# Every fourth weight block of the second half, while expert rows are gathered, loaded as two transfers of 104 and 24 partitions

## The chip, the cores and the metric

The kernel runs on one core of one Trainium2 chip. The metric is device time in microseconds of one execution; the median of three executions before the change is 2417.49 us (2416.55 to 2422.78).

## The reference

Two transformer layers in float32 on one sequence of 512 positions, width 1024. The first mixes with a gated delta rule and sparse attention, followed by a gated feed-forward part with a short convolution (width 2816). The second mixes with a pooling and a convolution branch, and then has an expert layer, which decides what follows here:

```python
q = (hc @ w_query).reshape(PEER_CHUNK, PEER_HEADS, PEER_KEY_DIM)      # 8 heads
...
experts = jnp.take_along_axis(cand_idx, pos, axis=-1)                 # 16 of 16384 per head
gate = jax.nn.softmax(top_s.astype(jnp.float32), axis=-1).astype(hc.dtype)
u = jnp.take(expert_u, experts, axis=0)
act = jax.nn.gelu(jnp.einsum('chkd,cd->chk', u, hc))
v = jnp.take(expert_v, experts, axis=0)
return jnp.einsum('chk,chkd->cd', gate * act, v)
```

Each of the 512 positions picks 8 x 16 = 128 experts, and of each the two rows u and v of 1024 floats are used. That is 512 x 128 x 8 KB = 537 MB to be read.

## The kernel before, in words

Positions are taken in two halves of 256. The first half runs ahead through the dense work of both layers; from about 940 us on the core gathers expert rows for its positions, and does the dense work of the second half (feed-forward up and down, `w_in_2`, `branch`, `w_out_2`, `query`) beside it.

The gather. `expert_u` and `expert_v` lie side by side in `experts`, so one indirect transfer brings for each of 128 positions one row of 8 KB, one row to each partition: 1 MB, 128 packets of 8 KB. There are 512 of them (4 tiles of 128 positions x 128 picks), issued by GpSimd in the last loop of its program (L2814) into `ring_e`, a ring of `RING` = 9 buffers. GpSimd waits before each until the row that had the buffer is used. A landed buffer is dotted with the position's vector on VectorE (`row_dot`, L2622), ScalarE makes the weight from it (L1761 to L1773), and the row is then summed on TensorE (`row_pair`) or, for some, on VectorE (`side_row`). Rows are taken in pairs; a pair is a step `p` of 0 to 255.

The dense blocks. `weight_order()` writes out by hand the order in which TensorE takes the weight blocks of the second half: block `t` of 0 to 191 is `ORDER[t]`, and `TURN` is the inverse. Which block stands after which pair is set by `UP_AT`, `DOWN_AT`, `WIN_AT`, `BRANCH_AT`, `WOUT_AT` and `QUERY_AT`. A block is 128 partitions x 1024 floats (512 KB), for eight of the `down` blocks 128 x 768 (384 KB). SyncE (SP) issues the loads in the order of `t` (L586 for `down`, L588 for the rest) into three slots (`SLOTS2` = 3, the tile `w2` in `ring`); slot `t % 3` is loaded again once TensorE has done block `t - 3` (`half_done`). TensorE waits in `weights(name, s, m)` on `slot_ready[t % 3]`, which each transfer raises by 16, before the block's matmuls. Blocks from 59 on belong to the steps of the gather.

TensorE's program is one sequence: for each pair first `row_pair(p, ...)` and then `beside(p)`, which holds the dense blocks. So a block that is late holds up the rows behind it, and a row that is late the blocks.

Of the kernel before, what the change touches and what calls it, by code (L numbers as in the profile page):

```python
# [32 lines left out]
SLOTS = 4  # L33
# [40 lines left out]
FIRST = {}  # L74
# [6 lines left out]
SLOTS2 = 3  # L81
# [64 lines left out]
def weight_order():  # L146

    order = [("w_out", 1, m) for m in range(SLOTS, KT)]
    order += [("w_in_2", 0, m) for m in range(28)] + [("branch", 0, m) for m in range(KT)]
    order += [("w_out_2", 0, m) for m in range(KT)] + [("up", 1, 0), ("up", 1, 1)]  # L150
    order += [("query", 0, m) for m in range(EARLY)] + [("up", 1, 2)]
    for p in range(NC * TILE):
        order += [("query", 0, m) for m, q in QUERY_AT[0].items() if q == p]
        order += [("up", 1, b) for b, q in enumerate(UP_AT) if q == p]
        order += [("down", 1, d) for d, q in enumerate(DOWN_AT) if q == p]
        order += [("w_in_2", 1, m) for m, q in enumerate(WIN_AT) if q == p]
        order += [("branch", 1, m) for m, q in enumerate(BRANCH_AT) if q == p]
        order += [("w_out_2", 1, m) for m, q in enumerate(WOUT_AT) if q == p]
        order += [("query", 1, m) for m, q in QUERY_AT[1].items() if q == p]
    return order  # L160


ORDER = weight_order()
TURN = {b: t for t, b in enumerate(ORDER)}


class Count:
# [29 lines left out]
def build(nc, a, out):  # L197
    ctx = ExitStack()
    with ctx:
# [106 lines left out]
        w2 = wring[:, 0:SLOTS2 * D].rearrange("p (j n) -> p j n", n=D)  # L306
# [61 lines left out]
        def sem(name):  # L368
            return ctx.enter_context(nc.semaphore(name))
# [135 lines left out]
        slot_ready = [sem(f"slot{j}_ready") for j in range(SLOTS)]  # L505
# [12 lines left out]
        def evicted(t):  # L518

            name, half, m = ORDER[t]  # L520
            if name == "w_out":
                return x1_ready, KT + m + 1
            if name == "w_in_2":
                return sg_ready, 28 * half + m + 1
            if name == "branch":
                return m_half, KT * half + m + 1
            if name == "w_out_2":
                return x3_ready, KT * half + m + 1
            if name == "up":
                return fy_ready, 2 * FT + m + 1  # L530
            if name == "down":
                return x2_ready, KT + m + 1
            return q_ready, 16 * half + m + 1
# [8 lines left out]
        def bank(name, half, m):  # L542
            if name == "w_out":
                return (4, 5, 6, 0)[m - SLOTS]
            return 2 + TURN[name, half, m] % SLOTS2

# [3 lines left out]
        @block.sync  # L550
        def _(sp):
            first = STREAM[0]
            sp.dma_start(crow, a["crow"][0]).then_inc(params_loaded, 16)
            sp.dma_start(const[:, 0:HEAD_CONST], a["const"][:, 0:HEAD_CONST]).then_inc(inputs_loaded, 16)
            sp.dma_start(xT[:], a["x"]).then_inc(inputs_loaded, 16)
            sp.dma_start(param[:], a["param"]).then_inc(rows_loaded, 16)
            sp.wait_ge(ada_used, 8)
            for j in range(SLOTS):
                sp.dma_start(ring[:, j, :D], a["w_in"][j]).then_inc(slot_ready[j], 16)
            sp.dma_start(const[:, HEAD_CONST:], a["const"][:, HEAD_CONST:]).then_inc(rest_loaded, 16)  # L560
            sp.dma_start(mats[:], a["mats"]).then_inc(rest_loaded, 16)
            for name, blocks, width in STREAM:
                lo = 1 if name == first[0] else 0
                with sp.Fori(lo, blocks // SLOTS) as i:
                    for j in range(SLOTS):

                        sp.wait_ge(blocks_done, FIRST[name] + i * SLOTS + j - SLOTS + 1)
                        if name == "down":
                            src = a[name][bass.ds(i * 2 + j // 2, 1)].rearrange("o p n -> p (o n)")[:, (j % 2) * WIDE:(j % 2 + 1) * WIDE]
                        else:  # L570
                            src = a["w_out" if name == "w_out_again" else name][bass.ds(i * SLOTS + j, 1)].rearrange("o p n -> p (o n)")
                        sp.dma_start(ring[:, j, :width], src).then_inc(slot_ready[j], 16)
            for t, (name, half, m) in enumerate(ORDER):

                if (name, half, m) == ("query", 1, KT):
                    sp.wait_ge(fin_ready, 1)
                    sp.dma_start(out[0], prow).then_inc(out_done, 16)

                if t < SLOTS2:
                    sp.wait_ge(blocks_done, FIRST["down"] + 13 + t)  # L580
                else:
                    sp.wait_ge(half_done, t - SLOTS2 + 1)
                if name == "down":
                    c, k = divmod(m, KT)
                    lo, hi = c * CHUNK * P, min(FT, (c + 1) * CHUNK) * P
                    sp.dma_start(w2[:, t % SLOTS2, 0:hi - lo], a[name][k][:, lo:hi]).then_inc(slot_ready[t % SLOTS2], 16)  # L586
                else:
                    sp.dma_start(w2[:, t % SLOTS2, :], a[name][m]).then_inc(slot_ready[t % SLOTS2], 16)  # L588
            for c in range(1, NC - 1):

                sp.wait_ge(fin_ready, c + 1)
                sp.dma_start(out[c], prow).then_inc(out_done, 16)
            for v in range(2):

                sp.wait_ge(fin_ready, NC + 1 + v)
                sp.dma_start(out[NC - 1][:, v * S:(v + 1) * S], prow[:, v * S:(v + 1) * S]).then_inc(out_done, 16)
            sp.wait_ge(out_done, 16 * (NC + 1))
# [3 lines left out]
        def _(pe):  # L601
# [280 lines left out]
            for c in range(NC):  # L882
                t = slice(c * P, (c + 1) * P)
# [125 lines left out]
            def weights(name, s, m):  # L1009

                t = TURN[name, s, m]
                pe.wait_ge(slot_ready[t % SLOTS2], 16 * (FIRST["down"] // SLOTS + 4 + t // SLOTS2 + 1))
                if t >= SLOTS2:
                    pe.wait_ge(*evicted(t - SLOTS2))
                return [w2[:, t % SLOTS2, k * P:(k + 1) * P] for k in range(KT)]

            def project_rest(m, lo=0, hi=KT):

                w = weights("w_out", 1, m)
                if m == KT - 1:  # L1020
                    pe.wait_ge(x2_ready, SLOTS + 1)
                for k in range(lo, hi):
                    ins = mm(PS[:, bank("w_out", 1, m), :HF], w[k], mix[:, k, HF:], k == 0, k == KT - 1)
                if hi == KT:
                    ins.then_inc(half_done, 1)

            def expand(m, lo=0, hi=KT):

                w = weights("up", 1, m)
                if m == 0:  # L1030
                    pe.wait_ge(h_ready, KT * 4)
                for k in range(lo, hi):
                    ins = mm(PS[:, bank("up", 1, m), :HF + 2], w[k], hf[:, k, :], k == 0, k == KT - 1)
                if hi == KT:
                    ins.then_inc(half_done, 1)

            def contract(c, m):

                w = weights("down", 1, c * KT + m)
                tiles_ = min(CHUNK, FT - c * CHUNK)  # L1040
                if m == 0:
                    pe.wait_ge(ff_ready, FT + c * CHUNK + tiles_)
                for k in range(tiles_):
                    ins = mm(PS[:, bank("down", 1, c * KT + m), :HF], w[k], gc[:, c % 2, k, :], k == 0, k == tiles_ - 1)
                ins.then_inc(half_done, 1)
# [47 lines left out]
            def branch_conv(s, m):  # L1093

                t = TURN["branch", s, m]
                if m == 0:
# [217 lines left out]
        def _(act):  # L1314
# [271 lines left out]
            def keep_block(s, m):  # L1586

                act.wait_ge(half_done, TURN["w_in_2", s, m] + 1)
                src = PS[:, bank("w_in_2", s, m), :HF]
# [56 lines left out]
            def up_tap(m):  # L1646

                t, z = divmod(m, 2)
                act.wait_ge(half_done, TURN["up", 1, m] + 1)
                if t >= 2:  # L1650
# [31 lines left out]
            def keep_query(s, m):  # L1682

                act.wait_ge(half_done, TURN["query", s, m] + 1)
                if 16 * s + m >= 2:
# [1256 lines left out]
```

## Time and profile before

| | us |
|---|---|
| median of three executions | 2417.49 (2416.55 to 2422.78) |
| the profiled execution's own time | 2412.99 |
| its span, first to last instruction | 2411.3 |
| TensorE busy | 2082.3 (86%) |
| VectorE busy | 1679.4 (70%) |
| ScalarE busy | 861.5 (36%) |
| GpSimd busy | 634.9 (26%) |
| expert rows moved by the gather, queue q0 (with other loads of GpSimd) | 588.90 MB |
| SyncE's transfers, queue q1 | 163.84 MB |

The profile gives for any stretch the busy time of each engine, the mean busy share of the core's 16 DMA engines and the bytes that they moved. A DMA share of 1.00 is all 16 busy; 0.06 is one of 16. Three kinds of queue matter: q0 is what GpSimd issues (here the expert rows), q1 what SyncE issues (here the weight blocks), q8 and q14 carry the program's own instructions to the engines.

### The profile page before, as it was taken

The page shows a single profiled execution, that of the slowest core. Times are in us where ns is not written, and L with a number is a line of the kernel's source. Part 1 is how long each engine was busy: PE and PEld are TensorE (multiplying, and loading weights), DVE is VectorE, ACT ScalarE, POOL GpSimd, SP SyncE. Part 2 cuts the span into 40 slices and gives each one's busy share as a digit, 9 for nine tenths or more (in the row PEclk, how much of TensorE's full clock was granted, in tenths as well). Part 3 has the DMA queues.
Part 4 walks back from the last instruction along what each step waited for, and adds up shares of the span by engine and source line. Part 5 has one row for each costly group of instructions (what it writes and reads, how often), then busy time and mean ns, then how long its engine had stood idle before and what let it go on. Part 6 is the DMA issues. An engine that isn't in the chain of part 4 may idle for free.

```text
span 2411.3 us, 26498 instructions
## 1 busy us (share of the span) xinstructions
PE 2082.3 (86%) x8832; PEld 1483.9 (62%) x8832; DVE 1679.4 (70%) x3760; ACT 861.5 (36%) x2094; POOL 634.9 (26%) x606
## 2 busy tenths in 40 slices
PE   7999998899999998999986878787788878777776
PEld 3444787788888887877765666676644423322322
DVE  5563645476657737999998999876676666676654
ACT  2321345421103213423326446356643333342332
POOL 2100000000110002333344334344444443444442
PEclk9999998999999999999997989899799999999999
DMA  8631120266774348999999999999999999999997
GB/s 350 197 121 55 34 71 1 105 225 228 259 282 147 133 157 326 412 417 415 418 416 420 407 379 402 399 398 420 420 420 421 421 421 422 419 421 419 421 422 292
DMA packets 131790, 754.31 MB, mean 313 GB/s; under 512 B 14544, under 2 KB 14672, under 8 KB 65616
## 3 DMA queue, kind: packets, MB, share of 16 engines
q0 software_dynamic: 87456, 588.90, 60.0%
q1 hardware_dynamic: 44208, 163.84, 18.7%
q8 instruction: 66, 1.08, 0.2%
q14 instruction: 60, 0.49, 0.1%
HBM read 750.59 MB, written 2.10 MB: 312 GB/s over the span
## 4 chain that ended last, share of the span: by engine, by line
PE 43%; DMA 31%; DVE 16%; ACT 5%; issue 3%; POOL 0%; DVEq 0%; SPq 0%; ACTq 0%; POOLq 0%
PE PS L603 41%; DMA arena<-experts_dram,ecur 25%; DVE arena L2622 5%; DVE arena L1891 4%; DVE h_all L1891 2%; DMA ring<-down_dram 2%; PE PS L1149 2%; DVE ring L1891 1%; DMA ring<-up_dram 1%; DVE arena L1885 1%; ACT L1761 1%; ACT arena L1765 1%; ACT arena L1771 1%; ACT const L1773 1%; DMA ring<-query_dram 1%
## 5 line engine op out<-in xcount | busy, mean ns | idle before, releaser
L603 PE MATMUL PS<-h_all,ring 128*128 128x256 f32 (+2 forms) x3584 | 895.9, 408 | 18.2 <-DMA ring<-up_dram 6.1
L2814 POOL DMA_INDIRECT arena<-experts_dram,ecur x512 | 585.8, 1144 | 1092.7 <-PE PS L1149 385.6
L2622 DVE CUSTOM_DVE_ANT_0 arena<-arena 128x1024 f32<-128x1024 f32 x512 | 626.1, 1223 | 282.8 <-DMA arena<-experts_dram,ecur 279.7
L603 PEld LDWEIGHTS PS<-h_all,ring 128*128 128x128 f32 x3584 | 681.1, 193 | 208.3 <-issue 102.8
L603 PE MATMUL PS<-arena,const 128*128 128x512 f32 (+1 forms) x1056 | 497.0, 618 | 135.7 <-ACT const L1773 125.1
L603 PEld LDWEIGHTS PS<-arena,const 128*128 128x128 f32 x1056 | 198.4, 196 | 418.5 <-issue 220.3
L1149 PE MATMUL PS<-const,arena 128*128 128x128 f32 x1304 | 196.6, 308 | 117.3 <-ACT arena L1771 113.4
L1761 ACT ACTIVATE arena<-arena 128x2 f32<-128x2 f32 x255 | 51.6, 202 | 659.4 <-DVE arena L2622 659.0
L1149 PEld LDWEIGHTS PS<-const,arena 128*128 128x128 f32 x1304 | 171.6, 159 | 143.4 <-ACT arena L1771 125.6
L603 PE MATMUL PS<-arena,ring 128*128 128x256 f32 x1088 | 245.9, 384 | 13.3 <-DMA ring<-down_dram 7.3
L603 PEld LDWEIGHTS PS<-arena,ring 128*128 128x128 f32 x1088 | 205.9, 192 | 47.8 <-DMA ring<-down_dram 12.8
L1771 ACT ACTIVATE arena<-arena 128x1024 f32<-128x1024 f32 x161 | 177.6, 1134 | 0.0
L603 PE MATMUL PS<-arena 128*128 128x128 f32 (+4 forms) x936 | 137.7, 299 | 8.4 <-DVE arena L1885 3.4
L603 PEld LDWEIGHTS PS<-arena 128*128 128x128 f32 (+2 forms) x936 | 117.9, 194 | 28.9 <-issue 12.8
L1891 DVE SCALAR_TENSOR_TENSOR arena<-arena 128x1024 f32<-128x1024 f32 (+3 forms) x132 | 125.8, 953 | 2.4
L1942 DVE CUSTOM_DVE_ANT_0 arena<-arena 128x1024 f32<-128x1024 f32 x92 | 108.9, 1222 | 25.1 <-DMA arena<-ada_dram 23.8
L1765 ACT ACTIVATE arena<-arena 128x1 f32<-128x1 f32 x510 | 122.4, 287 | 8.4
L1891 DVE SCALAR_TENSOR_TENSOR arena<-PS,param,arena 128x255 f32<-128x255 f32 (+3 forms) x128 | 72.3, 565 | 42.5 <-ACT arena L1392 31.6
L1891 DVE SCALAR_TENSOR_TENSOR xT<-PS,mod,xT 128x256 f32<-128x256 f32 x71 | 34.2, 482 | 79.9 <-PE PS L603 79.3
L1773 ACT ACTIVATE const<-const,arena 128x128 f32<-128x128 f32 x254 | 86.2, 387 | 0.0
L2794 POOL DMA_DIRECT2D arena<-crow_dram x1 | 0.5, 528 | 315.9 <-ACT arena L1556 315.9
L2801 POOL DMA_DIRECT2D arena<-ada_dram x44 | 23.2, 528 | 222.3 <-DVE mod L1942 209.5
(279 smaller groups left out, 1659.8 us busy)
## 6 DMA issues: line engine op xcount, KB each, us to landing
ring<-up_dram SPq DMA_DIRECT2D x88, 512.0 KB, 3.4
ring<-w_in_dram SPq DMA_DIRECT2D x80, 512.0 KB, 4.1
arena<-ada_dram POOLq DMA_DIRECT2D x80, 512.0 KB, 5.2
ring<-w_out_dram SPq DMA_DIRECT2D x32, 512.0 KB, 4.9
ring<-query_dram SPq DMA_DIRECT2D x32, 512.0 KB
ring<-down_dram SPq DMA_DIRECT2D x16, 704.0 KB, 5.9
ring<-branch_dram SPq DMA_DIRECT2D x16, 512.0 KB
arena<-experts_dram,ecur POOLq DMA_INDIRECT x512
```

The source lines that it names most:

```text
L603: return nc.tensor.matmul(o, l, r, start=start, stop=stop)
L1149: ins = nc.tensor.matmul(PS[:, k // 4, (k % 4) * P:(k % 4 + 1) * P], row[:, k * P:(k + 1) * P], ident, start=start and k % 4 == 0, stop=st ...
L1761: A(wts[:, b, :], dots[:, b, :], ACT.Gelu_apprx_tanh).then_inc(gelu_ready, 1)
L1765: A(wts[:, b, k:k + 1], wts[:, b, k:k + 1], ACT.Copy, scale=gcur[:, r % 3, j:j + 1]).then_inc(w_ready2, 1)
L1771: A(row, row, ACT.Copy, scale=wts[:, b, k:k + 1]).then_inc(row_scaled, 1)
L1773: A(diag[:, b, k, :], ident, ACT.Copy, scale=wts[:, b, k:k + 1]).then_inc(diag_ready if k == rows[-1] else act_step, 1)
L1885: return V.tensor_tensor(out=o, in0=x, in1=y, op=op)
L1891: return V.scalar_tensor_tensor(out=o, in0=x, scalar=s_, in1=y, op0=op0, op1=op1)
L1942: V.tensor_tensor_reduce(out=w, in0=w, in1=row, scale=1.0, scalar=0.0, op0=MUL, op1=ADD, accum_out=mod[:, blk, t:t + 1]).then_inc(used, 1)
L2622: V.tensor_tensor_reduce(out=u, in0=u, in1=hrow[:, (r // HEADS) % 2, :], scale=1.0, scalar=0.0, op0=MUL, op1=ADD, accum_out=dots[:, p % NB ...
L2801: pool.dma_start(ring_2[:, j, :], a["ada_2"][bass.ds(i * SLOTS + j, 1)].rearrange("o p n -> p (o n)")).then_inc(slot_2_ready[j], 16)
L2814: nc.gpsimd.indirect_dma_start(out=ring_e[:, g % RING, :], out_offset=None, in_=a["experts"], in_offset=bass.IndirectOffsetOnAxis(ap=ecur[ ...
```

## The change

A weight block with `t >= 59` and `t % 4 == 0` is loaded by two transfers, one for the partitions 0 to 103 and one for 104 to 127, into the same slot. Both raise the slot's semaphore by 16, and TensorE waits for the sum of all transfers of that slot so far. That is so for the 33 blocks t = 60, 64, ..., 188 of the 133 blocks from 59 on. Bytes, slots, the order of blocks and what TensorE does with them stay as they were.

```diff
+HEAD_PART = 104
+FIRST_SPLIT, EVERY = 59, 4
+
+
+def split(t):
+
+    return t >= FIRST_SPLIT and t % EVERY == 0
+
+
+def weight_landed(t):
+
+    return 16 * sum(1 + split(u) for u in range(t % SLOTS2, t + 1, SLOTS2))
...
-                    sp.dma_start(w2[:, t % SLOTS2, 0:hi - lo], a[name][k][:, lo:hi]).then_inc(slot_ready[t % SLOTS2], 16)
+                    w, src = w2[:, t % SLOTS2, 0:hi - lo], a[name][k][:, lo:hi]
                 else:
-                    sp.dma_start(w2[:, t % SLOTS2, :], a[name][m]).then_inc(slot_ready[t % SLOTS2], 16)
+                    w, src = w2[:, t % SLOTS2, :], a[name][m]
+                if split(t):
+                    sp.dma_start(w[0:HEAD_PART], src[0:HEAD_PART]).then_inc(slot_ready[t % SLOTS2], 16)
+                    sp.dma_start(w[HEAD_PART:], src[HEAD_PART:]).then_inc(slot_ready[t % SLOTS2], 16)
+                else:
+                    sp.dma_start(w, src).then_inc(slot_ready[t % SLOTS2], 16)
...
-                pe.wait_ge(slot_ready[t % SLOTS2], 16 * (FIRST["down"] // SLOTS + 4 + t // SLOTS2 + 1))
+                pe.wait_ge(slot_ready[t % SLOTS2], 16 * (FIRST["down"] // SLOTS + 4) + weight_landed(t))
```

## Rows read from the trace of the kernel before

**Rows 1.** Busy time by stretch: engines' busy us (instructions), TensorE clock, DMA share, GB/s.

```profile
940.00:1260.00 320.00, 291.39 (x1398) 244.58 (x1398) 299.04 (x620) 112.68 (x277) 115.57 (x91) 0.98 1.02 416
1260.00:1390.00 130.00, 95.28 (x500) 82.17 (x501) 117.07 (x275) 68.41 (x134) 48.56 (x44) 0.87 1.01 414
1390.00:1650.00 260.00, 204.97 (x1119) 178.50 (x1118) 225.12 (x529) 136.66 (x269) 106.56 (x85) 0.89 0.99 397
1650.00:1850.00 200.00, 157.34 (x673) 110.87 (x672) 132.89 (x340) 103.03 (x241) 83.00 (x72) 0.89 1.01 421
1850.00:2390.00 540.00, 421.83 (x950) 176.08 (x949) 354.85 (x859) 177.76 (x598) 223.62 (x213) 0.97 1.01 421
```

**Rows 2.** The DMA queues, 940 to 1260 us: packets, MB, share of 16 engines.

```profile
DMA packets 23701, 133.10 MB, mean 416 GB/s; under 512 B 2634, under 2 KB 2634, under 8 KB 12042
q0 software_dynamic: 13090, 95.34, 72.1%
q1 hardware_dynamic: 10590, 37.49, 29.1%
q8 instruction: 11, 0.18, 0.2%
```

**Rows 3.** The queues of SyncE and of the instructions, 1260 to 1390 us.

```profile
q1 hardware_dynamic: 2096, 7.60, 14.6%
q8 instruction: 4, 0.07, 0.2%
```

**Rows 4.** The same, 1390 to 1650 us.

```profile
q1 hardware_dynamic: 4751, 17.30, 16.7%
q8 instruction: 9, 0.15, 0.2%
```

**Rows 5.** The same, 1650 to 2390 us.

```profile
q1 hardware_dynamic: 2017, 7.34, 2.5%
q8 instruction: 13, 0.21, 0.1%
```

**Rows 6.** Busy time by stretch, the end of the gather, columns as in rows 1.

```profile
2380.00:2390.00 10.00, 6.66 (x15) 2.88 (x16) 5.00 (x9) 2.54 (x10) 2.30 (x2) 1.00 1.01 421
2390.00:2392.00 2.00, 0.74 (x2) 0.00 (x0) 0.77 (x3) 1.27 (x5) 0.00 (x0) 1.00 0.51 213
2392.00:2393.00 1.00, 0.99 (x3) 0.52 (x4) 1.00 (x1) 0.00 (x0) 0.00 (x0) 1.00 0.16 66
2393.00:2394.00 1.00, 1.00 (x4) 0.52 (x3) 0.09 (x2) 0.00 (x0) 0.00 (x0) 1.00 0.06 25
...
2398.00:2399.00 1.00, 1.00 (x4) 0.48 (x3) 0.03 (x2) 0.87 (x3) 0.00 (x0) 1.00 0.04 16
```

**Rows 7.** The queues, 2393.5 to 2399.2 us.

```profile
q0 software_dynamic: 20, 0.14, 5.9%
```

**Rows 8.** Instructions of VectorE's line L2622, 2370 to 2402 us, and what they waited for.

```profile
L2622 DVE CUSTOM_DVE_ANT_0 arena<-arena x12: 1224/1225/1226, 2371.0 to 2399.3; 128x1024 f32<-128x1024 f32 x12
...
  DMA arena<-experts_dram,ecur: 15.9, 12
```

**Rows 9.** Who waited for whom, 940 to 1260 us: us in total, times, longest.

```profile
POOL arena L2814 <- PE PS L1149: 164.9, 27, 16.9
...
PEld PS L603 <- DMA ring<-up_dram: 15.8, 22, 1.9
...
PEld PS L603 <- DMA ring<-down_dram: 12.8, 14, 1.8
...
```

**Rows 10.** SyncE's line L588, 940 to 1900 us: duration ns min/median/max.

```profile
L588 SPq DMA_DIRECT2D ring<-up_dram x39: 327/328/328, 955.1 to 1181.4; - x39
```

**Rows 11.** The chain that ended last, in order of time: start, us, what.

```profile
955.10 9.29 DMA ring<-up_dram
...
1646.38 16.92 DMA arena<-experts_dram,ecur
...
2396.95 6.29 PE PS L603 x14
```

## The prediction

> **What bounds the kernel now.** I read first the busy time by stretch [rows 1]. The reader is to see that from 940 us on the DMA engines are the full resource: share 1.01 to 1.02 and 414 to 421 GB/s in four stretches, and only 1390 to 1650 us has some air, with 397 GB/s. No other engine is full throughout: TensorE has 291 of 320 us in the first stretch and 422 of 540 in the last, VectorE 225 of 260 us in the middle one. The chain that ended last says the same [rows 11]: early on it goes through loads of weight blocks (9.3 us the one at 955 us), later through landings of expert rows (16.9 us the one at 1646 us).
>
> A mean share can hide that the 16 engines are not equally loaded, so next I read the end of the gather, where no new rows are issued [rows 6]. Up to 2390 us all 16 are busy. In 2390 to 2392 the share is 0.51, in the next microsecond 0.16, and from 2393 to about 2398.7 it is 0.06 or less at 25 GB/s: one engine of sixteen, alone for about 6 us, with 20 packets left [rows 7]. So one engine is some 6 us behind the rest, and the last rows wait for it: VectorE waited before each of its last 12 dot products for rows, 15.9 us in total, the last of them starts at 2399.3 [rows 8], and TensorE's last piece of 6.3 us ends behind it [rows 11].
>
> Why one? Every transfer of rows or weights ends with 16 small packets (2634 under 512 B over 91 gathers and 73 loads in 940 to 1260 us is 16.06 each [rows 2]; GpSimd's 91 instructions are the gathers [rows 1]), so all 16 engines take part in each and get 128/16 = 8 rows. What isn't spread is the instruction traffic: q8 had 11, 4, 9 and 13 packets of 16 KB in the four stretches [rows 2 to 5], 37 in all, of which each is one packet and so on one engine. The first 11 took 0.2% of 16 x 320 us, so about 0.93 us each (0.7 to 1.2 with the rounding). If all are on one engine it carries some 34 us more than the rest. At the end only 6 us of lag are left from the last 13 (12 us), since wherever the rest idle the late one catches up; 1390 to 1650 us is such a place. I take 6/13 = 0.46 us of lag per fetch as an estimate for the first stretches as well.
>
> **The change part by part.** SyncE's bytes in the four stretches [rows 2 to 5], at 0.524 MB a block (0.393 for eight, and 1.57 MB of results going out in the last), are some 73, 14, 32 and 11 loads. Counted back from the last block that is t = 62 to 191. So split ones are 18 in the first, 4 in the second, 8 in the third and 2 in the fourth; t = 60 is just before.
>
> *Issue.* Each split costs SyncE one more instruction of 0.33 us [rows 10], 33 x 0.33 = 11 us in all. SyncE has nothing but some 130 such issues in 900 us and waits for TensorE's blocks between them, so nothing is queued that this makes late; only the split block's second part starts 0.33 us later.
>
> *Packets.* A row of a block stays one packet of 4 KB, so 128 as before, with 16 more small ones. In 940 to 1260 us q1 took 29.1% of 16 x 320 us = 1490 us for 37.49 MB, that is 0.163 us per 4 KB packet; q0 took 72.1% for 95.34 MB, 0.317 us per 8 KB packet [rows 2].
>
> *Who moves them.* Neither 104 nor 24 divides by 16, so the load can't stay equal. The trace has no such transfer. Bounds: as evenly as it goes, an engine gets 7 + 2 = 9 rows at most in place of 8; at 8 rows an engine, as in a whole block, the 104 rows take 13 engines, and the 24 rows fall with 2 or 3 each on the first of the same, so 10 or 11 rows there and none on three engines. I take 10 rows on the busy ones and none on three, since 8 rows an engine is what the whole blocks have. Then a split adds 2 x 0.163 = 0.33 us to most engines and takes 8 x 0.163 = 1.3 us off three.
>
> The Trainium skill, page DMA: Bandwidth & Descriptors, section "Why a DMA increments its semaphore by 16 and not by 1", says that the number of engines is the largest one up to 16 that divides the outer dimension, the lowest-numbered ones: 13 for 104 rows and 12 for 24. By that rule engines 0 to 11 get 10 rows, engine 12 gets 8 and engines 13 to 15 none. No run here shows it yet.
>
> *940 to 1390 us.* DMA is full. 22 splits cost most engines 22 x 0.33 = 7.2 us (0 to 10.8 between no and three extra rows). The late engine has by then 15 fetches x 0.46 = 6.9 us of lag. If it is one of the three left out, it loses 22 x 1.3 = 29 us of work, lands with or before the rest, and the rest are 7.2 - 6.9 = 0.3 us later than the late one was. I take +0.3 us.
>
> *1390 to 1650 us.* 397 of 421 GB/s leaves 6% of 260 us, 15 us of air on each engine [rows 1], against 8 x 0.33 = 2.6 us: 0. If the cover were gone, +2.6 us.
>
> *From 1650 us.* Two splits. Most engines +0.65 us, which lies inside the 6 us in which they are idle at the end; the late one, if left out, 2 x 1.3 = 2.6 us less: -2.6 us, as its lag is what the end waits for.
>
> Sum: +0.3 + 0 - 2.6 = -2.3 us, on 2412.99 us of the profiled execution (its span and 1.7 us around it) 2410.7. The median of the runs lies 4.5 us above that execution, so in the terms of the median 2417.5 - 2.3 = 2415.2 us.
>
> **The rivals.** (a) *The late engine keeps its rows.* If it is one of those that get 10 rows, both the full stretches and the end are paid: 22 x 0.33 + 2 x 0.33 = +7.9 us, 2425.4 us. For it: twelve or thirteen of sixteen engines are such, and no view names the engine. Against: queues that carry instructions may lie on the high-numbered engines, of which nothing shows here. It decides as soon as the lone engine at the end is still there and about as long.
>
> The same page, section "Latency and other measured facts", says that engines 7 and 15 are usually the slower ones in traces. For 15 that gives the forecast, for 7 rival (a); rows 6 show one late engine and not two.
>
> (b) *Weight blocks land later and TensorE waits.* In 940 to 1260 us TensorE waited 36 times for an `up` or `down` block, 28.6 us together [rows 9], half of the 73 blocks. A split one has on most engines two more packets, each in turn with a row of q0: 2 x (0.163 + 0.317) = 0.96 us, and 0.33 us of issue. With half of 18 splits exposed, and what this pushes on the next blocks in the queue, 9 x 1.3 = 12 us: 2429 us. For it: the chain goes through these loads [rows 11]. Against: GpSimd waited 165 us for TensorE in that stretch [rows 9], rows are in stock, and DMA is full anyway, so what the weights lose the rows gain.
>
> (c) *The late engine sets the pace all along.* Then its relief counts in the first stretches in full, as lag there is nearer to 15 x 0.93 = 14 us than to 6.9: 7.2 - 14 = -6.8, and with up to -2.6 at the end -9.4 us: 2408 us. For it: 33 splits take 43 us off three engines, just about the 34 us of the fetches. Against: the share of DMA is 1.01, so the other fifteen don't idle for the late one before 1390 us.
>
> (d) *Nothing changes:* both parts are spread as before. The Trainium skill (same page, "Rules for kernel authors") says of two transfers to disjoint partition halves that they go through the same engines and bring nothing. That would be 2417.5 us. The odd sizes 104 and 24 speak against it here.
>
> **How the numbers follow.** Forecast, with (d) in it: 0.50. (a) 0.18, (b) 0.10, (c) 0.22. 0.3% of 2417.5 is 7.3 us, about what the runs can tell from no change: faster is under 2410.2, slower over 2424.8. Faster: (c) and a little less than its whole, 0.22. Slower: (a), of which a part stays inside 0.3%, and (b), 0.25. Same: the rest, 0.53. The range leaves out the far ends of (b) and (c): 2407 to 2427 us; the forecast's own is 2411 to 2420.
>
> **What would show it.** In the changed profile: SyncE's line of loads has 33 more instructions, 33 transfers of 416 KB (some 312) and 33 of 96 KB (72). Right: the stretch at the end with share 0.06 shrinks from 6 us to some 3, the rows from 1260 to 1390 us stay at the same times within 1 us, TensorE's waits for weight blocks stay near 29 us. Wrong: a lone engine for 6 us or more at the end and the whole gather some 8 us later (a); TensorE's waits for `up` and `down` blocks up by 10 us (b); the last gather landing 7 us or more earlier (c); DMA under 410 GB/s in the full stretches, which would say that uneven parts leave engines idle.

## The result, and the profile after

The changed kernel takes 2486.76 us (2485.8 to 2490.0, four runs) against 2418.66 us before (2416.55 to 2422.78): ratio 1.0286, 95% interval 1.0273 to 1.0299, so 68 us slower. The forecast was no measurable change, 2415.2 us in a range of 2407 to 2427 us. The profiled execution of the changed kernel has a span of 2488.3 us, 77.0 more than before. (That is more than 68 us because the profiled execution before lay 5.7 us under its median and this one 3.2 us over.)

First the same stretches as in [rows 1], of the changed kernel. The columns are the busy us (instructions) of TensorE's matmuls, its weight loads, VectorE, ScalarE and GpSimd, then TensorE's granted clock, the DMA share and GB/s.

```profile
940.00:1260.00 320.00, 264.35 (x1200) 222.47 (x1198) 258.77 (x538) 97.35 (x241) 92.86 (x76) 0.92 1.00 360
1260.00:1390.00 130.00, 97.08 (x464) 81.98 (x465) 109.10 (x239) 57.69 (x120) 55.66 (x42) 0.87 1.01 386
1390.00:1650.00 260.00, 197.07 (x1028) 170.10 (x1027) 230.55 (x541) 121.09 (x241) 90.44 (x77) 0.88 1.00 381
1650.00:1850.00 200.00, 147.86 (x811) 124.74 (x809) 128.09 (x318) 115.35 (x228) 80.87 (x69) 0.88 1.01 398
1850.00:2390.00 540.00, 432.94 (x1019) 190.74 (x1018) 365.50 (x919) 185.49 (x610) 226.18 (x211) 0.96 1.01 418
```

The reader is to see that the last two columns no longer go together. The DMA share is as full as before, but the rate fell from 416 to 360 GB/s in the first stretch, and to 386, 381 and 398 in the next three. The bytes missing are 56 x 320, 28 x 130, 16 x 260, 23 x 200 and 3 x 540 (in thousandths of a MB), 17.9 + 3.6 + 4.2 + 4.6 + 1.6 = 31.9 MB. At 421 GB/s that is 76 us, nearly the whole difference of the spans. So the DMA engines were busy and moved less: packets took longer. (The share of the first stretch fell a little, from 1.02 to 1.00; by that 2%, idle engines account for some 2.6 of its 17.9 MB, an estimate.)

The queues of the changed kernel in 940 to 1260 us (packets, MB, share of 16 engines), against [rows 2]:

```profile
q0 software_dynamic: 11293, 82.17, 69.6%
q1 hardware_dynamic: 9150, 32.81, 29.7%
```

An 8 KB packet took 0.696 x 5120 / (82.17 / 0.008192) = 0.355 us in place of 0.317, a 4 KB one 0.190 in place of 0.163. Both queues suffer, also the rows of experts, which the change doesn't touch.

One split stands nearly alone, the block t = 188, issued at 1857.55 us. The changed kernel in steps of 2 us from there, same columns:

```profile
1857.55:1859.55 2.00, 2.00 (x9) 1.04 (x8) 1.84 (x3) 0.56 (x3) 0.00 (x0) 1.00 0.99 414
1859.55:1861.55 2.00, 2.00 (x6) 0.92 (x5) 1.39 (x3) 1.45 (x5) 0.94 (x1) 1.00 1.05 412
1861.55:1863.55 2.00, 2.00 (x6) 0.93 (x5) 0.44 (x1) 0.00 (x0) 1.10 (x2) 1.00 1.01 299
1863.55:1865.55 2.00, 1.28 (x3) 0.21 (x2) 1.53 (x5) 0.26 (x2) 1.22 (x2) 1.00 1.09 309
1865.55:1867.55 2.00, 0.94 (x2) 0.49 (x3) 0.00 (x0) 1.98 (x5) 0.49 (x1) 1.00 0.99 274
1867.55:1869.55 2.00, 2.00 (x6) 0.95 (x5) 0.80 (x1) 0.62 (x3) 0.68 (x1) 1.00 0.99 389
1869.55:1873.55 4.00, 1.65 (x10) 0.99 (x8) 2.61 (x10) 1.00 (x1) 2.18 (x2) 1.00 1.01 420
```

For six microseconds, while the block's rows pass, the rate is some 290 GB/s at full share, then it climbs back to 420. The first 12 us carried 4.19 MB; an unsplit load at 1884.08 us left 5.03 MB in its 12 us. That is 0.84 MB or 2.0 us of DMA time for one split.

The packets of this block also tell how many engines move it. In the 12 us q1 had 153 packets, in those of the unsplit load 144, which are 128 rows and 16 small ones, one for each engine. 153 are 128 rows and 25 small ones: 13 engines for the 104 rows and 12 for the 24, the numbers that the prediction reckoned with.

TensorE's waits of the changed kernel in 940 to 1260 us, against [rows 9]:

```profile
PEld PS L621 <- DMA ring<-up_dram: 29.6, 14, 4.7
...
PEld PS L621 <- DMA ring<-down_dram: 12.9, 7, 3.9
PEld PS L621 <- DMA ring<-query_dram: 12.3, 4, 4.2
```

54.8 us in 25 waits, where before the same three had 30.0 us in 40 waits (28.6 in 36 for `up` and `down` [rows 9], 1.4 in 4 for `query`): fewer, but up to 4.7 us long in place of 1.9. By the line that issued the load, first the split blocks and then the whole ones:

```profile
  PEld PS L621: 47.5, 14
...
  PEld PS L621: 10.5, 12
```

Of the 15 split blocks in this stretch TensorE waited for 14, some 3.4 us each, and 0.9 us for a whole one.

And its end, against [rows 6]:

```profile
2469.00:2470.00 1.00, 1.00 (x3) 0.52 (x4) 1.00 (x1) 0.00 (x0) 0.00 (x0) 1.00 0.34 139
2470.00:2473.00 3.00, 2.70 (x7) 0.91 (x5) 1.32 (x4) 0.39 (x2) 0.00 (x0) 1.00 0.07 30
2473.00:2474.00 1.00, 0.07 (x1) 0.07 (x1) 0.22 (x1) 0.88 (x4) 0.00 (x0) 1.00 0.06 25
2474.00:2475.00 1.00, 1.00 (x3) 0.52 (x4) 1.00 (x2) 0.00 (x0) 0.00 (x0) 1.00 0.06 25
2475.00:2476.00 1.00, 1.00 (x4) 0.47 (x3) 0.02 (x2) 0.88 (x3) 0.00 (x0) 1.00 0.04 16
```

One engine still runs alone, for more than 5 us. The late engine was not relieved.

### The profile page after: what moved, and what is told of

Read it like the earlier page. It is cut to its first block, busy times and chain, and to the rows that moved or that the text cites. A ratio compares the mean times of both kernels' runs of the same rounds, so it can differ in the third digit from the quotient of the medians.

```text
span 2488.3 us, 26531 instructions
## 1 busy us (share of the span) xinstructions
PE 2111.3 (85%) x8832; PEld 1506.3 (61%) x8832; DVE 1681.3 (68%) x3760; ACT 861.4 (35%) x2094; POOL 632.9 (25%) x606
## 4 chain that ended last, share of the span: by engine, by line
PE 44%; DMA 34%; DVE 12%; ACT 6%; issue 3%; POOL 1%; SPq 0%; DVEq 0%; ACTq 0%; POOLq 0%
PE PS L621 42%; DMA arena<-experts_dram,ecur 24%; DVE arena L2640 4%; DMA ring<-up_dram 4%; DVE arena L1909 3%; DMA ring<-down_dram 3%; DVE h_all L1909 2%; PE PS L1167 2%; DMA ring<-query_dram 2%; ACT L1779 1%; ACT arena L1783 1%; DMA ring<-w_out_dram 1%; ACT arena L1789 1%; ACT const L1791 1%; DMA ring<-branch_dram 1%
## 5 line engine op out<-in xcount | busy, mean ns | idle before, releaser
L621 PE MATMUL PS<-h_all,ring 128*128 128x256 f32 (+2 forms) x3584 | 910.3, 413 | 46.2 <-DMA ring<-up_dram 24.4
L621 PEld LDWEIGHTS PS<-h_all,ring 128*128 128x128 f32 x3584 | 692.2, 196 | 239.7 <-issue 100.0
L621 PE MATMUL PS<-arena,const 128*128 128x512 f32 (+1 forms) x1056 | 502.9, 625 | 131.5 <-ACT const L1791 121.7
L621 PE MATMUL PS<-arena,ring 128*128 128x256 f32 x1088 | 251.2, 391 | 22.5 <-DMA ring<-down_dram 19.1
```

The costliest lines, as they stand in the source:

```text
L621: return nc.tensor.matmul(o, l, r, start=start, stop=stop)
```

## The experiments

Three theories stood against each other. **P**, displaced rows: in a transfer of 104 or 24 partitions most rows go out on another DMA engine than in one of 128; there they meet the packets of the engine that otherwise serves these partitions, and both get longer. **L**, load: ten rows on twelve engines in place of eight make those engines and the blocks late. **I**: each second transfer costs something by itself.

**Other cuts of the same 33 blocks.** One line each (`HEAD_PART = 112`, `96`, `64`), and a cut by columns:

```diff
-                    sp.dma_start(w[0:HEAD_PART], src[0:HEAD_PART]).then_inc(slot_ready[t % SLOTS2], 16)
-                    sp.dma_start(w[HEAD_PART:], src[HEAD_PART:]).then_inc(slot_ready[t % SLOTS2], 16)
+                    n_ = w.shape[1] // 2
+                    sp.dma_start(w[:, 0:n_], src[:, 0:n_]).then_inc(slot_ready[t % SLOTS2], 16)
+                    sp.dma_start(w[:, n_:], src[:, n_:]).then_inc(slot_ready[t % SLOTS2], 16)
```

> The changed kernel with parts of 112 and 16 partitions in place of 104 and 24: both divide by 16, so each engine still gets 7 + 1 = 8 rows of a split block, but other rows than in a whole block. Theory P (a row that goes out on another engine than in a whole block meets that partition's own engine on the way into SBUF, and both packets get longer): still much slower than before, +40 to +90 us, 8 KB packets well over 315 ns in the first stretch. Theory L (10 rows on twelve engines in place of 8 make them, and the weight blocks, late): the load is even again, within 5 us of before. Theory I (the second transfer itself costs, by its issue or its completion): about +70 us as with the change.

> Parts of 96 and 32 partitions: 6 + 2 = 8 rows for each engine. Theory P: +40 to +90 us. Theory L: within 5 us of before. Theory I: about +70 us.

> Parts of 64 and 64 partitions: 4 + 4 = 8 rows for each engine. Theory P: slower, +20 to +90 us, unless the engines happen to get the rows that they have in a whole block. Theory L: within 5 us of before. Theory I: about +70 us.

> The same 33 blocks as two transfers, but cut by columns: all 128 partitions in each, rows of 2 KB. Every row stays on its engine, each engine has 16 packets of 2 KB in place of 8 of 4 KB. Theory P: within 6 us of before. Theory L: within 6 us of before. Theory I: about +70 us.

Measured against 2415.88 us: 112 + 16 2459.44 us (ratio 1.0179, 1.0153 to 1.0205), 96 + 32 2461.38 (1.0189, 1.0165 to 1.0213), 64 + 64 2474.18 (1.0247, 1.0221 to 1.0274), columns 2439.50 (1.0103, 1.0077 to 1.0129). So cuts in which every engine keeps eight rows cost 44, 45 and 58 us: L alone can't be it. In the first stretch 112 + 16 ran at 381 GB/s and 64 + 64 at 373, both at a DMA share of 1.02, as full as before. The column cut cost 24 us where P and L said under 6, and theory I said 70: a miss for all three, and it needed a reason of its own. First stretch of the column cut:

```profile
940.00:1260.00 320.00, 276.70 (x1304) 234.87 (x1304) 282.15 (x587) 104.89 (x257) 106.18 (x84) 0.96 0.98 393
```

Here the share falls as well (0.98 from 1.02): part of the loss is idle engines. After 1260 us the column cut runs at 415, 393, 420 and 421 GB/s, as before [rows 1].

**Where the splits stand.** `FIRST_SPLIT = 135` (14 splits, none in the first stretch) for 104 + 24 (p135), for 112 + 16 (m135) and for columns (c135); the columns only before t = 135 (cfirst, 19 splits); every eighth block in place of every fourth (ev8, 16 splits).

> 104 + 24 only for blocks from t = 135 on (14 splits in place of 33), so none in the stretch in which TensorE waits for weight blocks. Theory P (displaced rows stretch the packets; some 2.0 us of DMA time per split, from the one split that stands alone in the changed trace: 4.19 MB in 12 us in place of 5.04): 14 x 2.0 = +28 us. Theory L (late weight blocks hold up TensorE) gives next to nothing here: under +6 us.

> 112 + 16 for the 14 blocks from t = 135 on. Each engine has 8 rows again. If the stretched packets are all of the cost (1.53 us lost by a pair that stands alone), 14 x 1.5 = +21 us, against +25 us measured for 104 + 24 in the same places. If the unevenness (10 rows on twelve engines) is most of the cost of 104 + 24 here, under +10 us.

> The split by columns only for blocks from t = 135 on. If the 23.6 us of the column split came from weight blocks that take 16 turns beside the expert rows in place of 8, while TensorE waits for them (940 to 1260 us), this costs under +4 us. If each second transfer costs 0.7 us wherever it stands (theory I), 14 x 0.7 = +10 us.

> The split by columns only for the blocks before t = 135 (19 splits). All 33 cost 23.6 us and the 14 from 135 on 1.3 us. If the cost lies in the blocks that TensorE waits for, with 16 turns of an engine in place of 8, it is all here: +19 to +25 us, and TensorE's waits for up, down and query blocks in 940 to 1260 us are well above the 29 us of before.

> 104 + 24 for every eighth block (16 splits in place of 33), over all stretches. If the cost is one per split, about half of the change's 68 to 70 us: +32 to +36 us. If it comes from the balance between engines or from TensorE waiting in single places, another share.

| | splits | us, before | ratio (95%) | us more | per split |
|---|---|---|---|---|---|
| p135 | 14 | 2442.10, 2416.85 | 1.0102 (1.0085 to 1.0119) | 25.3 | 1.8 |
| m135 | 14 | 2430.60, 2415.64 | 1.0065 (1.0049 to 1.0082) | 15.0 | 1.1 |
| c135 | 14 | 2418.18, 2416.85 | 1.0005 (0.9995 to 1.0015) | 1.3 | 0.1 |
| cfirst | 19 | 2442.14, 2415.64 | 1.0110 (1.0093 to 1.0127) | 26.5 | 1.4 |
| ev8 | 16 | 2449.88, 2416.85 | 1.0137 (1.0121 to 1.0154) | 33.0 | 2.1 |

c135 rules out I: 14 more transfers cost nothing measurable where TensorE hardly waits for blocks (6.6 us of such waits in 1260 to 1900 us). All of the column cut's cost lies before t = 135. The waits of cfirst there:

```profile
PEld PS L622 <- DMA ring<-up_dram: 22.6, 15, 5.4
...
PEld PS L622 <- DMA ring<-down_dram: 15.8, 9, 3.5
...
PEld PS L622 <- DMA ring<-query_dram: 8.9, 3, 5.0
```

47.3 us in 27 waits, against 30.0 in 40 before, and the DMA share of the stretch is 0.96. If the queues take turns, with an 8 KB packet of rows between two packets of the block, then 16 packets of 2 KB an engine in place of 8 of 4 KB need 16 x (0.317 + 0.08) = 6.4 us in place of 3.8 (an estimate from the packet times of [rows 2]). The trace of cfirst has the times from issue to landing of its loads in this stretch, first the second halves, then the whole blocks:

```profile
DMA to landing us min/median/max: 6.7/10.2/12.2
...
DMA to landing us min/median/max: 3.3/8.4/11.7
```

The second half is issued 0.37 us after the first, so a cut block is complete some 2.2 us later than a whole one, near the 2.6 us of the estimate. Then TensorE, the reuse of its row buffers, and in the end the DMA engines wait. ev8 came out at half the change's cost, as expected. p135 came near the 28 us that the lone split gave for P, where L said under 6. m135 was expected at 21 for P and came out at 15: what is left between it and p135, 10 us, belongs to the uneven cut. In the probes below a 104 + 24 pair loses 0.31 us more than a 112 + 16 pair, so 14 x 0.31 = 4.4 us; the two more rows an engine, 14 x 0.33 = 4.6 us, would be most of the rest. That last part was not measured alone.

**Shapes one by one.** The kernel before, with loads of weight rows into the weight slots after the last block is done, beside nothing but the gather, one every 20 us:

```diff
+                for p, parts in PROBES[c]:
+                    sp.wait_ge(rows_used, by_tensor(BATCH * p))
+                    if probe_n:
+                        sp.wait_ge(slot_probe, 16 * probe_n)
+                    for lo, hi in parts:
+                        sp.dma_start(w2[lo:hi, probe_n % SLOTS2, :], a["up"][probe_n][lo:hi]).then_inc(slot_probe, 16)
+                        probe_n += 1
```

> The kernel before with 25 more loads of weight rows (4 KB each, 1696 rows, 6.95 MB, results unused) into the free weight slots once the last weight block is done, each alone beside the gather, some 20 us apart: partitions 0-127, 0-103, 104-127, 0-111, 112-127, 0-95, 96-127, 0-63, 64-127, 0-127, 0-119, 120-127, then pairs (104+24, 112+16, 64+64), then 0-31, 0-15, 0-7, 24-127, 0-127, 0-103, 104-127. Theory P: the 12 us after a whole one carry some 5.03 MB, those after 104, 112, 96 or 64 rows lose 0.4 to 0.9 MB at full DMA share, also 112, 96 and 64 where every engine has the same number of rows, and small ones lose in proportion to their rows. A theory in which the number of engines or the evenness of their load decides: 112, 96, 64, 32 and 16 lose nothing, 104, 120, 24 and 8 do. Time: 6.95 MB at 421 GB/s is 16.5 us, and with P some 15 us more.

The whole kernel took 2455.71 us (1.0159, 1.0138 to 1.0179). The 12 us after each issue, columns as above; in order 104 + 24, 112 + 16, 64 + 64, partitions 0-7, 0-127, 0-103, 104-127 (the diff leaves out the table of loads; the kernel has 25 of them):

```profile
2196.77:2208.77 12.00, 7.40 (x16) 2.87 (x16) 5.15 (x13) 2.42 (x10) 5.18 (x5) 1.00 1.02 355
2220.10:2232.10 12.00, 7.40 (x16) 2.88 (x16) 6.15 (x14) 4.02 (x13) 5.74 (x5) 1.00 1.01 366
2244.01:2256.01 12.00, 7.40 (x16) 2.88 (x16) 5.35 (x12) 2.12 (x9) 5.70 (x6) 1.00 1.01 345
...
2308.70:2320.70 12.00, 7.40 (x16) 2.88 (x16) 7.18 (x19) 5.80 (x17) 4.72 (x5) 1.00 1.01 408
2352.99:2364.99 12.00, 7.40 (x16) 2.87 (x16) 6.13 (x13) 4.91 (x13) 5.95 (x6) 1.00 1.02 421
2373.98:2385.98 12.00, 7.40 (x16) 2.88 (x16) 4.45 (x7) 2.42 (x10) 4.69 (x5) 1.00 1.01 372
2396.72:2408.72 12.00, 7.40 (x16) 2.88 (x16) 5.12 (x9) 3.56 (x14) 5.60 (x6) 1.00 1.01 397
```

Of these only the whole one keeps 421 GB/s. The pair of the change loses 66 x 12 = 0.79 MB or 1.9 us, 112 + 16 1.6 us, 64 + 64 2.2 us; each part alone loses too (104: 1.4 us, 24: 0.7 us), and even eight rows, 32 KB, lose 0.16 MB, five times what they carry. The twelve single loads that came first, from 1913 us on, agree: two whole ones left 423 GB/s, the cut ones 367 (0-119) to 406 (112-127 and 120-127), with 371 for 0-103 and 397 for 104-127. The whole run took 39 us more, where 16.5 us for the bytes and some 15 for P were expected.

By the lone pair 33 x 1.9 = 63 us of the 68. That this comes so near is in part luck: the same product gives 52 us for 112 + 16 and 72 for 64 + 64, where 44 and 58 were measured. If the lone pair overstates the even cuts and 104 + 24 alike, displaced rows make some 52 us of the 68 (an estimate), and the uneven load of the engines is the nearest reason for the rest.

**The same number of rows, on their own engines.** As the last one, with a step between the partitions (`w2[lo:hi:by, ...]`):

> Again loads of 4 KB rows into the free weight slots late in the gather, each alone, now with a step between partitions. Eight rows to partitions 0, 4, ..., 28 go out on the engines 0 to 7, and if in a whole block engine e has the partitions 4e to 4e+3 and 32+4e to 35+4e, each of these rows is on its own engine; so are 1, 5, ..., 29 and 32, 36, ..., 60, and 0, 4, 8, 12 on four engines. Rows 0-7 in a row (two engines' partitions served by eight) and 64, 68, ..., 92 (each on the wrong engine, but one to one) are not. Order: 0-31 step 4, 0-7, 1-31 step 4, 32-63 step 4, 64-95 step 4, 0-3, 0-15 step 4, 0, 4, 64, 0-63 step 4, 0-127 step 8; then 0-31 step 4, 96-127 step 4, 120-127, 64-95 step 4, 0-127, 0-31, 0-127 step 4, 32-63 step 4, 0-7, 0. Theory P: those on their own engines lose nothing (under 0.03 MB in 12 us), those displaced do: 0-7 some 0.16 MB as measured for it before, 64-95 step 4 also loses, 0-63 step 4 and 0-127 step 8 lose more. If few engines or the unevenness did it, 0-31 step 4 would lose what 0-7 loses.

2423.43 us (1.0038, 1.0022 to 1.0054). In order: 0-7 without a step, 1-31 step 4, 32-63 step 4, 64-95 step 4, 0-63 step 4, 0-127 step 8, 0-31 step 4, 120-127 (with nothing added this run's stream gives 419 to 423 GB/s):

```profile
1919.20:1931.20 12.00, 9.62 (x21) 4.15 (x21) 7.31 (x25) 6.71 (x20) 5.47 (x5) 0.86 1.01 412
1925.88:1937.88 12.00, 9.46 (x24) 3.97 (x23) 8.69 (x25) 3.90 (x16) 6.01 (x5) 1.00 1.01 421
1944.96:1956.96 12.00, 8.05 (x18) 3.29 (x19) 7.86 (x17) 3.68 (x15) 4.94 (x5) 1.00 1.01 421
1965.01:1977.01 12.00, 7.82 (x17) 3.18 (x18) 8.16 (x26) 5.02 (x16) 5.85 (x5) 1.00 1.01 414
...
2086.94:2098.94 12.00, 7.55 (x17) 3.26 (x18) 8.10 (x26) 5.97 (x18) 5.22 (x5) 1.00 1.01 405
2107.16:2119.16 12.00, 8.26 (x21) 3.68 (x22) 7.63 (x17) 4.14 (x16) 5.19 (x5) 1.00 1.01 412
2179.98:2191.98 12.00, 8.09 (x18) 3.33 (x19) 7.50 (x16) 3.68 (x15) 5.16 (x5) 1.00 1.01 422
...
2221.17:2233.17 12.00, 7.68 (x17) 3.16 (x18) 7.08 (x16) 3.65 (x15) 4.68 (x5) 1.00 1.01 408
```

Eight rows in one transfer cost nothing measurable when they are 0, 4, ..., 28 or 1, 5, ..., 29 or 32, 36, ..., 60. They cost when they are 64, 68, ..., 92 (414 GB/s, and 416 the second time), 96, 100, ..., 124 (414), 120 to 127 (408) or 0 to 7 (412). Each of these loads has 16 packets, eight rows and eight small ones, so eight engines. Number of transfers, rows, engines and bytes are the same; only which rows they are differs. That is what P says, and it rules out that few engines or odd numbers are the reason. Two things stay open. The trace doesn't name the engine of a packet. And row n of the source always goes to partition n here, so the source rows differ with the partitions; against them as the reason speaks that the gather's own source rows are picked by the data, so that on that side no engine has rows of its own.

Two later loads of this run, the whole block at 2263.32 us (399 GB/s) and 0-7 at 2346.62 us (402), stood where the rate had begun to fall before their issue (365 GB/s in 2262 to 2264 us, 352 and 315 in 2342 to 2346 us); 0-127 step 4 at 2305.36 us (395) can't be told apart from such a fall either. Falls of this kind come without any displaced row too: 348 GB/s at share 0.91 in c135 (2258 to 2262 us), 352 at 0.95 in low4 (2296 to 2300 us). Each follows a few microseconds in which TensorE's granted clock was 0.57 to 0.72; what makes them is not known.

The Trainium skill agrees: the page DMA: Bandwidth & Descriptors, section "The descriptor swizzle", gives for a whole transfer engine e (0 to 7) the partitions 4e to 4e+3 and 32+4e to 35+4e and engines 8 to 15 those from 64 on, each engine one port of SBUF; the page SBUF — State Buffer, section "Door 1: The DMA port swizzle (why `[64,N]` ≈ `[32,N]`)", has the same sets as ports. The free and the costly sets above fall just so: 0, 4, ..., 28 are one row for each of the engines 0 to 7 at its own place, 64, 68, ..., 92 one row for each at the place of another. That it is the port at which the packets meet is read from this map; the runs show which partitions cost, not where in the path.

**Which engine is late.** Forty loads of eight rows (0, 4, ..., 28: engines 0 to 7) beside 80 of the last gathers (low8), and forty of four rows (0, 4, 8, 12: engines 0 to 3), with `(0, 16, 4)` in the same line (low4):

```diff
+PROBES = {1: [], 2: [(210 + i, [(0, 32, 4)]) for i in range(40)]}
```

> The kernel before with 40 loads of eight rows (partitions 0, 4, ..., 28, engines 0 to 7) beside the last 80 gathers: 40 x 0.163 = 6.5 us more work for engines 0 to 7. If the engine that is late at the end is one of these, the end moves by about that: +6 us, and the lone engine runs for some 6 us as before. If it is one of 8 to 15, the end stays within 2 us and the stretch with one busy engine shrinks, as seven or eight others are now as late.

> As with the eight rows on engines 0 to 7 late in the gather (which moved the end by 8.4 us and left the lone engine 6 us behind the others), now four rows, partitions 0, 4, 8 and 12, on the engines 0 to 3. If the late engine is one of 0 to 3 the end moves by +6 to +8 us again; if it is one of 4 to 7, by under 2 us.

2424.19 us (1.0035, 1.0023 to 1.0046) and 2422.87 us (1.0035, 1.0022 to 1.0047), 8.4 and 7.2 us more. The end with four rows:

```profile
2398.00:2400.00 2.00, 0.73 (x3) 0.21 (x2) 0.77 (x3) 1.27 (x5) 0.00 (x0) 1.00 0.29 119
2400.00:2406.00 6.00, 4.76 (x11) 1.90 (x11) 3.33 (x6) 1.42 (x6) 0.00 (x0) 1.00 0.07 30
2406.00:2407.00 1.00, 1.00 (x4) 0.40 (x3) 0.00 (x0) 0.74 (x3) 0.00 (x0) 1.00 0.02 8
```

The end moved by the added 6.5 us or a little more, and the lone engine is still alone for 6 us. Had the late engine been another, the end should have moved by under 2 us, with four or five engines busy last. The loads of low4 have eight packets, four rows and four small ones, so four engines. Which four is not seen. Taking the engines of a transfer from the lowest up (the Trainium skill's rule quoted in the prediction, page DMA: Bandwidth & Descriptors, section "Why a DMA increments its semaphore by 16 and not by 1"; the small packets bear out its numbers of engines, the costly and free sets fit the order), the late engine is one of 0 to 3, not one of those that 104 + 24 leaves out.

## Why the prediction was wrong

*What bounds the kernel.* Right: DMA is full, and bytes lost in it come out one to one (31.9 MB, 76 of 77 us).

*Packets.* This is the step that failed. It took "0.163 us per 4 KB packet" and "0.317 us per 8 KB packet" from the kernel before and kept them for a transfer of which it said itself that the trace has no such one. The count of rows was right (the small packets are 9 more for a split, not 16), their durations were not: 0.190 and 0.355 us over the first stretch. In the bound for it I varied only how many rows an engine gets, not whether a packet takes as long on another engine. The missing term is 1.9 us for a split that stands alone, 63 us for all by that product, and some 52 if it overstates this cut as it does the even ones.

*Who moves them.* 13 and 12 engines, as reckoned: the 25 small packets of a split show it. The term for it, 0.33 us a split or 11 us for all 33, is small beside the missing one. The whole difference between 104 + 24 and 112 + 16 is 68 - 44 = 24 us for 33 splits and 10 us for 14; it holds this term and was not split further.

*940 to 1390 us.* Forecast +0.3. Missing bytes are 17.9 + 3.6 = 21.5 MB, 51 us. The 19 splits before t = 135 cost 68 - 25 = 43 us or 2.3 each, more than the 1.9 of a lone pair. That TensorE waits longer there is seen. As the DMA share stayed at 1.00, most of the loss is in longer packets; how much of the 43 us the later blocks add is not settled.

*1390 to 1650 us.* Forecast 0, behind 15 us of air: 4.2 MB less, 10 us. The air was mostly not there. I read it from the rate, 397 of 421 GB/s, but the share was 0.99 against 1.01 to 1.02 beside it, so only 5 to 8 us were idle (estimate); and p135 lost 25 GB/s there (372) while its share stayed at 0.99.

*From 1650 us.* Forecast -2.6 by the relief of the late engine: it is among 0 to 3 (by the rule above) and got more rows, and 4.6 + 1.6 = 6.2 MB are missing, 15 us. This is the fact that rival (a) needed, but its price (+7.9) was a ninth of what came.

*Rival (b)*, late weight blocks, does exist, and cfirst shows it nearly alone: 26.5 us for 19 blocks that land some 2.2 us later. It was priced at 12. *Rival (c)* needed a relieved late engine, which there was not, so its pace argument was not tried by the change. (In low4 the 6.5 us added to four engines came out in full at the end, while the three beside the late one were hardly behind: share 0.29 for 2 us and then one alone. That fits a late engine that holds the pace there.) *Rival (d)* cited the "don't bother" of the Trainium skill (page DMA: Bandwidth & Descriptors, section "Rules for kernel authors"); the reason given there, that both parts go through the same engines, led me to "no change", where the measured answer is a loss. The last sign I named, DMA under 410 GB/s, came (360), but the reading that I gave it, that engines are left idle, was wrong: at share 1.00 they were busy with stretched packets.

## What to carry to other kernels

When DMA is the full resource, cut a transfer so that every row stays on the engine that the whole transfer gives it: by columns, or not at all. Here a cut by columns cost nothing measurable while nothing waited for it (c135) and 1.4 us a block while TensorE did, because the cut block landed later. Where the rate falls at a full DMA share, look at the mean packet (share x 16 x time / packets), not only at the load of the engines. Such a fall over a few microseconds is no proof of displaced rows, since some came without any.

## What the runs showed that I had not expected

Eight displaced rows of 4 KB, 32 KB in all, take 0.16 MB of room from a stream of 421 GB/s (0.11 MB the second time, 0-7 both times), and a whole block in halves of 64 partitions 0.91 MB; eight rows on their own engines take nothing measurable. And one engine, by low4 one of 0 to 3, ends the gather 5 to 6 us after the other fifteen in every one of these kernels whose end was read, which I take for the 37 instruction fetches, but which no run shows as their work.
